# Sums over tokens and backward offsets placed among the exponents and inner products of the SSD outputs, exponent rows loaded in two halves

## The chip, the cores and the metric

The program runs on one core of a Trainium2 chip. The metric is the device time of one execution in microseconds; of several runs the median counts. The profile is of one execution, and its times are microseconds from the start of its span.

## What is computed

Two blocks run one after the other over 2048 tokens of width 1024. The first mixes by pooling and by a bidirectional state space scan (SSD), the second by a linear recurrence and by forgetting attention. The change touches only the stage that computes the outputs of the SSD. With 16 heads of width 64 in 4 groups, states of size 128 and chunks of 128 tokens, the reference says for each direction:

```python
acum = jnp.cumsum(adt, axis=2)
seg = acum[:, :, :, None] - acum[:, :, None, :]
decay = jnp.exp(jnp.where(lower, seg, -jnp.inf))
cb = jnp.einsum('bclgn,bcsgn->bclsg', cc, bc)
y_diag = jnp.einsum('bclsg,bclsgr,bcsgrp->bclgrp', cb, decay, xd)
chunk_states = jnp.einsum('bclgn,bclgr,bclgrp->bcgrpn', bc, decay_to_end, xd)
y_off = jnp.einsum('bclgn,bcgrpn,bclgr->bclgrp', cc, h_starts, jnp.exp(acum))
y = y_diag + y_off
```

and the output is `y_f + flip(y_b) + d_skip * xs`, multiplied by a gate. `h_starts` is the state at the start of each chunk: the state before times a decay, plus `chunk_states`.

## The kernel before

`ssd` goes over 16 chunks (`NC`), one function for each engine, and the order of the work on each engine is written out by hand. Semaphores are counted up by the steps and waited for by number. The backward states come from memory (`h_bwd`); the forward states are made here.

**TensorE, chunk c**, in its order of code:
- `products(c + 2)`: four 128x128 products of B and C into `psCB`, which is one of the two buffers of the exponents (`psE`). It waits until all exponentials of chunk c+1 are taken.
- `offset(c, hf)`: four products of 256 columns of C with the forward state into `psO`. It waits for `off_b_read`, since `psO` is one buffer and VectorE must have read the backward offsets of chunk c-1 from it.
- `skipped(0)`, a product of 512 columns with the identity into `psY`, then the inner products of heads 0 to 3 (`inside`, 64 columns each), and from there alternately `ahead(q)`, which is `exponents(c + 2, q)`, and two heads of `inside`. Each `exponents` is two products of 512 columns into `psE`: one over 10 rows (`seg_l`, `seg_r`), one with the masks. `skipped(1)` stands between `ahead(2)` and `ahead(3)`.
- `offset(c, hb)`, the same for the backward state, again into `psO`. It waits for `off_f_read`.
- `sums(c + 1)`, four products of 256 columns of B with the weighted inputs `xw` into `psS`. It waits for `weighted` (GpSimd), for the load of B, and for `state`: VectorE must have read `psS` of chunk c.

An fp32 product is recorded as two matmuls, so that the four of `offset` or `sums` are x8 in a row of the trace.

**VectorE, chunk c**: `state(c)` (line 919 decays the state into `y_tmp`, line 923 adds `psS` and counts up `state`), `decays(c + 1)` (lines 927 and 931, 2048 columns each), `forward(c)` (line 937 reads the forward offsets and counts up `off_f_read`; line 941 adds `psY`, once `inside` is counted up), `backward(c)` (line 944 reads the backward offsets, once `off_b` is counted up, and counts up `off_b_read`; line 948 adds them). In odd chunks line 964 follows, a piece of the next stage's weights.

**GpSimd, chunk c**: `weighted(c + 1)` (line 828), `gated(c - 1)` (line 838), in odd chunks a piece of weights (line 864), `skip(c + 1)` (line 834, which waits until `inside` of chunk c is done), and then `load_rows(c + 3)` (lines 841 and 843: three DMAs that bring the cumulated rows of both directions for the exponents). **ScalarE** takes the exponentials (line 888), copies `psCB` (line 877), and in odd chunks makes a part of the weights (line 909). **SyncE** issues the loads: `load_xs(c + 2)`, the inputs, when `inside` of chunk c is done, and the backward state of chunk c+2 when `off_b` of chunk c is.

## Time and profile before

| | us |
|---|---|
| median of 3 runs | 3515.5 |
| the runs | 3512.1, 3523.51, 3515.5 |
| the profiled execution, its own time | 3511.33 |
| its span | 3509.4 |
| TensorE busy in the span | 3265.5 (93%) |
| VectorE busy | 1642.1 (47%) |
| ScalarE, GpSimd busy | 962.8 (27%), 383.8 (11%) |
| granted TensorE clock, mean of the span | 0.95 |

The profiled execution is 4.2 us under the median and inside the spread of the runs; 1.9 us of its time lie outside the span. The granted clock is told as a share of full speed: 1.00 is 2.4 GHz, 0.50 is 1.2 GHz. Busy time of TensorE is not time at its peak, since matmuls are pipelined: a short matmul that waits for its weights counts as busy too.

### The profile page before, as it was taken

The page shows a single profiled execution, that of the slowest core. Times are in us where ns is not written, and L with a number is a line of the kernel's source. Part 1 is how long each engine was busy: PE and PEld are TensorE (multiplying, and loading weights), DVE is VectorE, ACT ScalarE, POOL GpSimd, SP SyncE. Part 2 cuts the span into 40 slices and gives each one's busy share as a digit, 9 for nine tenths or more (in the row PEclk, how much of TensorE's full clock was granted, in tenths as well). Part 3 has the DMA queues.
Part 4 walks back from the last instruction along what each step waited for, and adds up shares of the span by engine and source line. Part 5 has one row for each costly group of instructions (what it writes and reads, how often), then busy time and mean ns, then how long its engine had stood idle before and what let it go on. Part 6 is the DMA issues. An engine that isn't in the chain of part 4 may idle for free. (4 is left out here: it accounts for less than half of the span.)

```text
span 3509.4 us, 37796 instructions
## 1 busy us (share of the span) xinstructions
PE 3265.5 (93%) x15012; PEld 2564.9 (73%) x15012; DVE 1642.1 (47%) x1887; ACT 962.8 (27%) x1795; POOL 383.8 (11%) x246
## 2 busy tenths in 40 slices
PE   7899999997999979996999969999999699999788
PEld 7688888876888857765888858888877355555567
DVE  2754452466014237874444443243243665554355
ACT  2412221111210144532222231233223234433210
POOL 0100000000012035553000000000000201010012
PEclk9999999999999978987999989999999699999899
DMA  4222223332226355544333341222223312210232
GB/s 163 69 77 59 95 87 130 127 131 85 85 94 218 103 160 161 166 129 148 116 114 119 108 165 62 92 92 95 68 89 86 91 37 49 60 37 7 104 112 96
DMA packets 210926, 358.43 MB, mean 102 GB/s; under 512 B 22030, under 2 KB 143502, under 8 KB 202899
## 3 DMA queue, kind: packets, MB, share of 16 engines
q1 hardware_dynamic: 197782, 332.72, 29.3%
q10 hardware_dynamic: 5616, 17.97, 1.4%
q0 software_dynamic: 7392, 5.82, 0.8%
q8 instruction: 98, 1.61, 0.2%
q14 instruction: 38, 0.31, 0.0%
HBM read 234.57 MB, written 121.74 MB: 102 GB/s over the span
## 5 line engine op out<-in xcount | busy, mean ns | idle before, releaser
L636 PE MATMUL p_ps<-hmT_hi,p_w_hi 128*128 128x512 f32 x1312 | 525.5, 401 | 22.0 <-ACT p_work L356 16.4
L636 PE MATMUL p_ps<-hmT_hi,p_w_lo 128*128 128x512 f32 x1312 | 514.8, 392 | 0.0
L636 PE MATMUL p_ps<-hmT_lo,p_w_hi 128*128 128x512 f32 x1312 | 513.9, 392 | 0.0
L1748 PE MATMUL p_ps<-h2T_hi,p_w_hi 128*128 128x512 f32 x800 | 327.9, 410 | 19.2 <-DVE h2T_lo L1607 19.2
L1748 PE MATMUL p_ps<-h2T_hi,p_w_lo 128*128 128x512 f32 x800 | 315.6, 395 | 0.0
L1748 PE MATMUL p_ps<-h2T_lo,p_w_hi 128*128 128x512 f32 x800 | 315.4, 394 | 0.0
L636 PEld LDWEIGHTS p_ps<-hmT_hi,p_w_hi 128*128 128x128 f32 x1312 | 248.7, 190 | 75.9 <-issue 21.6
L636 PEld LDWEIGHTS p_ps<-hmT_hi,p_w_lo 128*128 128x128 f32 x1312 | 248.1, 189 | 53.4
L636 PEld LDWEIGHTS p_ps<-hmT_lo,p_w_hi 128*128 128x128 f32 x1312 | 248.9, 190 | 49.6
L1907 PE MATMUL t_psO<-t_prob,t_v 128*65 128x512 f32 (+3 forms) x640 | 262.0, 532 | 0.9
L1964 ACT ACTIVATE t_prob<-t_psS 128x1024 f32<-128x1024 f32 (+1 forms) x160 | 150.0, 938 | 317.7 <-PE t_psS L1895 179.5
L2002 DVE TENSOR_REDUCE t_chunk_max<-t_psM 128x1 f32<-128x512 f32 (+2 forms) x320 | 182.2, 606 | 94.9 <-PE t_psM L1878 70.0
L1748 PEld LDWEIGHTS p_ps<-h2T_hi,p_w_hi 128*128 128x128 f32 x800 | 153.0, 191 | 56.2 <-issue 24.6
L462 DVE COPY p_work<-p_ps 128x512 f32<-128x512 f32 (+3 forms) x93 | 55.6, 631 | 294.2 <-PE p_ps L656 260.5
L1748 PEld LDWEIGHTS p_ps<-h2T_lo,p_w_hi 128*128 128x128 f32 x800 | 152.6, 191 | 36.6 <-issue 6.0
L1748 PEld LDWEIGHTS p_ps<-h2T_hi,p_w_lo 128*128 128x128 f32 x800 | 152.4, 191 | 32.7
L1878 PE MATMUL t_psM<-t_KM,t_QB 66*128 66x512 f32 (+2 forms) x320 | 131.5, 479 | 27.2 <-DVE t_mask_k L2062 23.7
L1894 PE MATMUL t_psS<-t_QA,t_KA 128*128 128x512 f32 (+1 forms) x320 | 146.2, 457 | 9.3 <-DMA t_QB<-t_max_lo 9.2
L1907 PEld LDWEIGHTS t_psO<-t_prob,t_v 128*65 128x65 f32 x640 | 83.5, 138 | 96.5 <-issue 80.8
L1601 DVE TENSOR_TENSOR p_w_lo<-p_w_raw,p_w_hi 128x1024 fp32r<-128x1024 f32 x25 | 37.4, 1496 | 241.1 <-ACT p_w_hi L1503 241.1
L447 DVE TENSOR_TENSOR p_w_lo<-p_w_raw,p_w_hi 128x1024 fp32r<-128x1024 f32 x41 | 51.1, 1245 | 162.2 <-ACT p_w_hi L320 162.1
L1895 PE MATMUL t_psS<-t_QB,t_KB 68*128 68x512 f32 (+1 forms) x320 | 120.5, 376 | 0.0
(365 smaller groups left out, 5875.9 us busy)
## 6 DMA issues: line engine op xcount, KB each, us to landing
p_w_raw<-in_w_in SPq DMA_DIRECT2D x66, 512.0 KB, 6.0
p_spare<-in_wada ACTq DMA_DIRECT2D x32, 512.0 KB, 4.9
p_spare<-scratch_xs_tok SPq DMA_DIRECT2D x19, 512.0 KB, 4.4
scratch_xs_tok<-p_work SPq DMA_DIRECT2D x8, 1152.0 KB, 6.1
p_work<-in_wada SPq DMA_DIRECT2D x16, 512.0 KB, 3.4
p_work<-in_x SPq DMA_DIRECT2D x16, 512.0 KB, 3.3
scratch_dT<-p_work SPq DMA_DIRECT2D x8, 1024.0 KB, 5.9
scratch_zpT<-p_work SPq DMA_DIRECT2D x8, 1024.0 KB, 4.0
```

Source lines behind the costliest of these rows:

```text
L447: v.tensor_tensor(w_lo[b % 2][:], w_raw[b % 2][:], w_hi[b % 2][:].bitcast(F32), ALU.subtract).then_inc(S["w_lo"], 1)
L462: v.tensor_copy(tok_of(b)[:, 4 * g:4 * g + cnt, 0:width], tiles(PS[:, bank, :])[:, 0:cnt, 0:width]).then_inc(S["group_read"], 1)
L636: mm = pe.matmul(PS[:, c, 0:width], wt[n][:, q, :], xx[:, q, cols], start=(q == 0 and j == 0), stop=(q == KT - 1 and j == 2))
L1601: v.tensor_tensor(w_lo[b % 2][:], w_raw[b % 2][:], w_hi[b % 2][:].bitcast(F32), ALU.subtract).then_inc(S["w_lo"], 1)
L1748: mm = pe.matmul(ps[:, c, :], wt[n][:, q, :], xx[:, q, c * CH:(c + 1) * CH], start=(q == 0 and j == 0), stop=(q == KT - 1 and j == 2))
L1878: mm = pe.matmul(psM[:, m % 2, 0:w], QB[n][0:KM_ROWS, j * P:(j + 1) * P], KM[n][:, c * CH:c * CH + w], start=True, stop=not edge, skip_gro ...
L1894: pe.matmul(out, KA[n][:, ks], QA[n][:, qs], start=True, stop=False, skip_group_check=True)
L1895: mm = pe.matmul(out, KB[n][:, ks], QB[n][:, qs], start=False, stop=not edge, skip_group_check=True)
L1907: mm = pe.matmul(psO[:, o:CH], va[n][:, kt + e, 0:VD], pt[p % 2][:, e, o:CH], start=(kt + e == 0), stop=(kt + e == 4 * qc + 3), skip_group ...
L1964: act.activation(pt[p % 2][:, :, off:CH], psS[p % 2][:, :, off:CH], ACT.Exp, scale=1.0 / 8).then_inc(S["prob"], 1)
L2002: v.reduce_max(mx[:, j, c:c + 1], psM[:, m % 2, 0:w], axis=AX_X).then_inc(S["first_read"], 1)
```

## The change

The four products of `sums(c + 1)` no longer stand together at the end of chunk c. One stands after each of `ahead(1)`, `ahead(2)`, `ahead(4)` and `ahead(5)`; the first of them carries the waits. The four products of the backward offset are cut into two pairs, one before the last two heads and one after `ahead(7)`; the first pair carries the waits, the second counts up `off_b`. `load_rows` loads the rows of one direction at a time, and `exponents` waits for the first half at q = 0 and for the second at q = 4, each with its own semaphore. GpSimd issues the first half before `skip(c + 1)` (as soon as `ahead(3)` is done) and the second half after it.

```diff
@@ -754,10 +754,11 @@
         k = kit
         S = k.sems("y_", ("cb", "cb_copied", "weighted", "summed", "state", "seg", "exp", "skip",
                           "merged", "decays", "inside", "off_f", "off_f_read", "forward", "off_b", "off_b_read", "summed_y",
-                          "gated", "const", "lndt_in", "rows_in", "gate_in", "masks_in", "const_in", "seg_in", "z_in", "w_in", "w_gated", "w_hi",
+                          "gated", "const", "lndt_in", "rows_in", "gate_in", "masks_in", "const_in", "z_in", "w_in", "w_gated", "w_hi",
                           "w_lo"))
         bT_in, bt_in, x_in, h_in, y_out = ([k.sem(f"y_{what}{n}") for n in range(2)] for what in
                                            ("bT_loaded", "b_loaded", "xs_loaded", "hb_loaded", "stored"))
+        seg_in = [k.sem(f"y_seg_rows_loaded{n}") for n in range(2)]
         cT_in = [k.sem(f"y_cT_loaded{n}") for n in range(4)]
         dve = Tally(k.sem("y_dve_chain"))
         tokens = lambda t, c: t[c * P:(c + 1) * P, :]
@@ -836,22 +837,24 @@
                     g.wait_ge(S["summed_y"], c + 1)
                     g.wait_ge(S["z_in"], 16 * (c + 1))
                     g.tensor_tensor(y[c % 2][:], y[c % 2][:], zt[:], ALU.mult).then_inc(S["gated"], 1)
-                def load_rows(c):
-                    both = a["acum_rows"][:, c:c + 1]
-                    g.dma_start(seg_r[0:2, :], both.rearrange("m o h l -> m (o h l)")).then_inc(S["seg_in"], 16)
+                def load_rows(c, d):
+                    both = a["acum_rows"][:, c:c + 1, d * HEADS:(d + 1) * HEADS]
+                    g.dma_start(seg_r[0:2, d * HEADS * P:(d + 1) * HEADS * P],
+                                both.rearrange("m o h l -> m (o h l)")).then_inc(seg_in[d], 16)
                     for m in range(2):
-                        g.dma_start(seg_l[2 + 4 * m:6 + 4 * m],
-                                     both[m].rearrange("o (q j) l -> j (o q) l", j=4)).then_inc(S["seg_in"], 16)
+                        g.dma_start(seg_l[2 + 4 * m:6 + 4 * m, 4 * d:4 * d + 4],
+                                    both[m].rearrange("o (q j) l -> j (o q) l", j=4)).then_inc(seg_in[d], 16)
                 g.dma_start(seg_r[2:10], a["seg_r"][2:10]).then_inc(S["const_in"], 16)
                 g.dma_start(seg_l[0:2], a["seg_l"][0:2]).then_inc(S["const_in"], 16)
-                load_rows(0)
+                load_rows(0, 0)
+                load_rows(0, 1)
                 g.wait_ge(S["rows_in"], 80)
                 weighted(0)
                 skip(0)
-                g.wait_ge(S["seg"], 8)
-                load_rows(1)
-                g.wait_ge(S["seg"], 16)
-                load_rows(2)
+                for c in range(1, 3):
+                    for d in range(2):
+                        g.wait_ge(S["seg"], 8 * (c - 1) + 4 * d + 4)
+                        load_rows(c, d)
                 for c in range(NC):
                     if c + 1 < NC - 1:
                         weighted(c + 1)
@@ -862,11 +865,14 @@
                     if c % 2 == 1:
                         g.wait_ge(S["w_in"], 16 * (c // 2 + 1))
                         g.tensor_tensor(piece[:], piece[:], w.gate[:], ALU.mult).then_inc(S["w_gated"], 1)
+                    if c + 3 < NC:
+                        g.wait_ge(S["seg"], 8 * (c + 2) + 4)
+                        load_rows(c + 3, 0)
                     if c + 1 < NC:
                         skip(c + 1)
                     if c + 3 < NC:
                         g.wait_ge(S["seg"], 8 * (c + 3))
-                        load_rows(c + 3)
+                        load_rows(c + 3, 1)
                 gated(NC - 1)
             @block.scalar
             def _(act):
@@ -974,8 +980,8 @@
                         mm = pe.matmul(psCB[:, g, :], bT[c % 2][:, g, :], cT[c % 4][:, g, :], start=True, stop=True)
                     mm.then_inc(S["cb"], 1)
                 def exponents(c, q):
-                    if q == 0:
-                        pe.wait_ge(S["seg_in"], 48 * (c + 1))
+                    if q % 4 == 0:
+                        pe.wait_ge(seg_in[q // 4], 48 * (c + 1))
                     if q == 1:
                         pe.wait_ge(S["cb_copied"], c + 1)
                     elif 8 * c + q >= 2:
@@ -984,17 +990,19 @@
                               start=True, stop=False)
                     pe.matmul(psE[:, q % 2], ident_r[:], tri_r[:, q // 4].unsqueeze(1).to_broadcast([P, 4, P]), start=False,
                               stop=True).then_inc(S["seg"], 1)
-                def sums(c):
-                    pe.wait_ge(S["weighted"], c + 1)
-                    pe.wait_ge(bt_in[c % 2], 16 * (c // 2 + 1))
-                    if c >= 1:
-                        pe.wait_ge(S["state"], c)
-                    for g in range(GROUPS):
+                def sums(c, groups):
+                    if groups[0] == 0:
+                        pe.wait_ge(S["weighted"], c + 1)
+                        pe.wait_ge(bt_in[c % 2], 16 * (c // 2 + 1))
+                        if c >= 1:
+                            pe.wait_ge(S["state"], c)
+                    for g in groups:
                         mm = pe.matmul(psS[:, g * 256:(g + 1) * 256], bt[c % 2][:, g * NS:(g + 1) * NS],
                                        xw[:, g * 256:(g + 1) * 256], start=True, stop=True)
-                    mm.then_inc(S["summed"], 1)
-                def offset(c, state):
-                    for g in range(GROUPS):
+                    if groups[-1] == GROUPS - 1:
+                        mm.then_inc(S["summed"], 1)
+                def offset(c, state, groups=range(GROUPS)):
+                    for g in groups:
                         mm = pe.matmul(psO[:, g * 256:(g + 1) * 256], cT[c % 4][:, g, :], state[:, g * 256:(g + 1) * 256],
                                        start=True, stop=True)
                     return mm
@@ -1013,7 +1021,7 @@
                     for q in range(8):
                         exponents(c, q)
                     if c == 0:
-                        sums(0)
+                        sums(0, range(GROUPS))
                 pe.wait_ge(S["rows_in"], 80)
                 for c in range(NC):
                     ahead = (lambda q: exponents(c + 2, q)) if c + 2 < NC else (lambda q: None)
@@ -1030,25 +1038,29 @@
                     skipped(0)
                     inside(c, range(0, 4))
                     ahead(0)
+                    beside = (lambda g: sums(c + 1, (g,))) if c + 1 < NC - 1 else (lambda g: None)
                     inside(c, range(4, 6))
                     ahead(1)
+                    beside(0)
                     inside(c, range(6, 8))
                     ahead(2)
+                    beside(1)
                     skipped(1)
                     ahead(3)
                     inside(c, range(8, 10))
                     ahead(4)
+                    beside(2)
                     inside(c, range(10, 12))
                     ahead(5)
+                    beside(3)
                     inside(c, range(12, 14))
                     ahead(6)
+                    pe.wait_ge(S["off_f_read"], c + 1)
+                    pe.wait_ge(h_in[c % 2], 16 * (c // 2 + 1))
+                    offset(c, hb[c % 2], (0, 1))
                     inside(c, range(14, 16)).then_inc(S["inside"], 1)
                     ahead(7)
-                    pe.wait_ge(S["off_f_read"], c + 1)
-                    pe.wait_ge(h_in[c % 2], 16 * (c // 2 + 1))
-                    offset(c, hb[c % 2]).then_inc(S["off_b"], 1)
-                    if c + 1 < NC - 1:
-                        sums(c + 1)
+                    offset(c, hb[c % 2], (2, 3)).then_inc(S["off_b"], 1)
 def walk_tiles(eng, body, tally=None, per=0):
     body(0, 0)
     with eng.Fori(0, LT // 2 - 1) as i:
```

TensorE, from the skip product of a chunk to the second skip product. `psSeg` is the tile of the exponents, `psY` that of the inner and skip products, `psSt` that of the sums, `psO` that of the offsets. Before:

```order
4654 L1002 MATMUL psY<-y_xskip,ident 128x512
4655 L1006 MATMUL psY<-y_xs,y_decay_f 128x64 x4
4656 L983 MATMUL psSeg<-y_seg_r,y_seg_l 128x512
4657 L985 MATMUL psSeg<-y_masks_r,y_ident 128x512
4658 L1006 MATMUL psY<-y_xs,y_decay_f 128x64 x2
4659 L983 MATMUL psSeg<-y_seg_r,y_seg_l 128x512
4660 L985 MATMUL psSeg<-y_masks_r,y_ident 128x512
4661 L1006 MATMUL psY<-y_xs,y_decay_f 128x64 x2
4662 L983 MATMUL psSeg<-y_seg_r,y_seg_l 128x512
4663 L985 MATMUL psSeg<-y_masks_r,y_ident 128x512
4664 L1002 MATMUL psY<-y_xskip,ident 128x512
```

TensorE in the changed kernel, from the first inner products of a chunk to the same place:

```order
4642 L1014 MATMUL psY<-y_xs,y_decay_f 128x64 x4
4643 L989 MATMUL psSeg<-y_seg_r,y_seg_l 128x512
4644 L991 MATMUL psSeg<-y_masks_r,y_ident 128x512
4645 L1014 MATMUL psY<-y_xs,y_decay_f 128x64 x2
4646 L989 MATMUL psSeg<-y_seg_r,y_seg_l 128x512
4647 L991 MATMUL psSeg<-y_masks_r,y_ident 128x512
4648 L1000 MATMUL psSt<-y_xw,y_b 128x256
4649 L1014 MATMUL psY<-y_xs,y_decay_f 128x64 x2
4650 L989 MATMUL psSeg<-y_seg_r,y_seg_l 128x512
4651 L991 MATMUL psSeg<-y_masks_r,y_ident 128x512
4652 L1000 MATMUL psSt<-y_xw,y_b 128x256
4653 L1010 MATMUL psY<-y_xskip,ident 128x512
```

The first product of the sums now stands behind eight inner products and two exponents of its chunk, and everything that follows it in TensorE's queue waits for what it waits for.

TensorE, the end of a chunk and the start of the next. Before:

```order
4647 L1006 MATMUL psY<-y_xs,y_decay_f 128x64 x2
4648 L983 MATMUL psSeg<-y_seg_r,y_seg_l 128x512
4649 L985 MATMUL psSeg<-y_masks_r,y_ident 128x512
4650 L998 MATMUL psO<-y_hb,y_cT 128x256 x4
4651 L993 MATMUL psSt<-y_xw,y_b 128x256 x4
4652 L974 MATMUL psSeg<-y_cT,y_bT 128x128 x4
4653 L998 MATMUL psO<-y_hf,y_cT 128x256 x4
```

TensorE at the same place in the changed kernel:

```order
4667 L1006 MATMUL psO<-y_hb,y_cT 128x256 x2
4668 L1014 MATMUL psY<-y_xs,y_decay_f 128x64 x2
4669 L989 MATMUL psSeg<-y_seg_r,y_seg_l 128x512
4670 L991 MATMUL psSeg<-y_masks_r,y_ident 128x512
4671 L1006 MATMUL psO<-y_hb,y_cT 128x256 x2
4672 L980 MATMUL psSeg<-y_cT,y_bT 128x128 x4
4673 L1006 MATMUL psO<-y_hf,y_cT 128x256 x4
```

Between the last write of the backward offsets and the first write of the next forward offsets, both into `psO`, stood eight products; now four stand there, the small ones.

## Rows read from the trace of the kernel before

**Rows 1.** Busy time by stretch, the 13 chunks between two reads of backward offsets; columns first.
```profile
core 0: us, PE busy (x) PEld busy (x) DVE busy (x) ACT busy (x) POOL busy (x), PEclk, DMA share, GB/s
1293.90:1561.50 267.60, 267.50 (x1093) 196.37 (x1093) 207.67 (x111) 133.59 (x436) 152.49 (x84) 0.86 0.50 153
```

**Rows 2.** The same view, chunks 9, 10 and 11, each from skip product to skip product.
```profile
1464.70:1482.60 17.90, 17.90 (x86) 13.23 (x86) 15.95 (x9) 10.75 (x34) 13.38 (x7) 1.00 0.50 155
1482.60:1505.20 22.60, 22.60 (x86) 16.56 (x85) 17.62 (x12) 9.72 (x33) 9.37 (x7) 0.77 0.58 173
1505.20:1526.20 21.00, 21.00 (x85) 15.38 (x84) 13.72 (x7) 10.76 (x34) 15.04 (x9) 0.84 0.40 131
```

**Rows 3.** The same view, cut where the granted clock changes: chunk 7, then chunk 14.
```profile
1421.10:1430.10 9.00, 9.00 (x41) 5.72 (x39) 8.90 (x4) 5.34 (x20) 7.90 (x3) 1.00 0.59 175
1430.10:1440.40 10.30, 10.30 (x27) 7.83 (x27) 5.17 (x5) 4.81 (x15) 3.63 (x4) 0.50 0.28 69
...
1573.50:1577.00 3.50, 0.00 (x0) 0.00 (x0) 3.50 (x2) 0.00 (x0) 0.29 (x1) 0.50 0.00 0
```

**Rows 4.** Timeline of TensorE, chunk 9: start us, us, engine, line, instruction, tiles.
```profile
1464.75 1.02 PE L1002 MATMUL psY<-y_xskip,ident 128*128 128x512 f32 x2
...
1468.55 0.55 PE L1006 MATMUL psY<-y_xs,y_decay_f 128*128 128x64 f32 x4
...
1476.50 1.89 PE L998 MATMUL psO<-y_hb,y_cT 128*128 128x256 f32 x8
...
1479.95 1.05 PE L974 MATMUL psSeg<-y_cT,y_bT 128*128 128x128 f32 x8
1480.84 1.89 PE L998 MATMUL psO<-y_hf,y_cT 128*128 128x256 f32 x8
1482.57 1.02 PE L1002 MATMUL psY<-y_xskip,ident 128*128 128x512 f32 x2
```

**Rows 5.** Timeline at the tail, chunks 14 and 15; in brackets the idle time before.
```profile
1580.72 1.22 DVE L944 TENSOR_TENSOR y_tmp<-psO,y_eac 128x1024 f32<-128x1024 f32 x1 [2.39 <-PE psO L998]
...
1582.09 1.97 PE L998 MATMUL psO<-y_hf,y_cT 128*128 128x256 f32 x8 [1.41 <-DVE y_tmp L944]
```

**Rows 6.** Timeline of VectorE from the backward read of chunk 9.
```profile
1478.43 1.23 DVE L944 TENSOR_TENSOR y_tmp<-psO,y_eac 128x1024 f32<-128x1024 f32 x1 [1.28 <-PE psO L998]
...
1480.83 2.92 DVE L964 SCALAR_TENSOR_TENSOR wo_early_lo<-y_w_piece,cols,wo_early_hi 128x1024 fp32r<-128x1024 f32 x1
...
1487.10 1.22 DVE L923 TENSOR_TENSOR y_hf<-y_tmp,psSt 128x1024 f32<-128x1024 f32 x1
```

**Rows 7.** The same view from the backward read of chunk 7.
```profile
1438.60 1.23 DVE L944 TENSOR_TENSOR y_tmp<-psO,y_eac 128x1024 f32<-128x1024 f32 x1 [3.57 <-PE psO L998]
...
1441.00 1.28 DVE L964 SCALAR_TENSOR_TENSOR wo_early_lo<-y_w_piece,cols,wo_early_hi 128x1024 fp32r<-128x1024 f32 x1
...
1445.16 1.22 DVE L923 TENSOR_TENSOR y_hf<-y_tmp,psSt 128x1024 f32<-128x1024 f32 x1
```

**Rows 8.** The same view from the backward read of chunk 8.
```profile
1460.20 1.23 DVE L944 TENSOR_TENSOR y_tmp<-psO,y_eac 128x1024 f32<-128x1024 f32 x1 [3.57 <-PE psO L998]
...
1465.56 1.22 DVE L923 TENSOR_TENSOR y_hf<-y_tmp,psSt 128x1024 f32<-128x1024 f32 x1
...
1474.18 1.21 DVE L937 TENSOR_TENSOR y_out<-psO,y_eac 128x1024 f32<-128x1024 f32 x1
```

**Rows 9.** Timelines of GpSimd: chunks 7 and 9.
```profile
1441.40 2.64 POOL L828 TENSOR_TENSOR y_xw<-y_xs,y_wst 128x1024 f32<-128x1024 f32 x1 [3.92 <-PE psSt L993]
...
1475.96 1.90 POOL L834 TENSOR_TENSOR y_xskip<-y_xs,y_dskip 128x1024 f32<-128x1024 f32 x1 [3.85 <-PE psY L1006]
1480.27 2.40 POOL L828 TENSOR_TENSOR y_xw<-y_xs,y_wst 128x1024 f32<-128x1024 f32 x1 [0.67 <-PE psSt L993]
```

**Rows 10.** Loads of the tile y_xs, issued 14 times from 1291.3 to 1556.6.
```profile
DMA to landing us min/median/max: 3.3/3.5/5.0
```

**Rows 11.** Waits from 1281 to 1589: who waited, for whom, us in total, times, longest.
```profile
PEld psSeg L983 <- DMA y_seg_l<-scratch_acum_rows: 0.2, 1, 0.2
```

## The prediction

> **What bounds the kernel now.** I read the busy time by stretch first. In the 13 chunks between the backward read of chunk 0 and that of chunk 13 TensorE is busy for 267.50 of 267.60 us [rows 1], so the stage is TensorE's, and nothing there can be won by taking waits away. But the granted clock of the stretch is 0.86. Next the same view chunk by chunk: chunk 9 runs at clock 1.00 and takes 17.9 us, chunk 10 has 0.77 and takes 22.6, chunk 11 has 0.84 and takes 21.0, with the same work [rows 2]. This repeats every three chunks. Cut where the clock changes, chunk 7 shows 9.0 us at 1.00 and then 10.3 at 0.50, in which TensorE was never idle [rows 3]: the clock fell among the exponents and inner products, and came back during the long run of offsets, sums and products. So the prize is the clock. A low stretch of 10.3 us made chunk 10 dearer by 22.6 - 17.9 = 4.7 us, one of 21.0 - 17.9 = 3.1 us belongs to 0.16 x 21.0 / 0.5 = 6.7 us low: 0.46 us for each us at the low clock. Over the 13 chunks 0.14 x 267.6 / 0.5 = 75 us are low, which cost 75 x 0.46 = 34 us. That is the most that the change can take, and 13 chunks at 17.9 are 233 us. The other engines are next: VectorE is busy for 15.95 of 17.9 us in the full-speed chunk [rows 2].
>
> **The rows in halves** cost or bring nothing. TensorE waited for exponent rows 0.2 us in the whole stage [rows 11]. Three more issues by GpSimd in each chunk stand ahead of `skip`, where GpSimd idles anyway: 3.85 us before line 834 in chunk 9 [rows 9], against 1.7 us that three issues take (below). If that cover is gone, `skip` comes later by up to 1.7 us, and its 1.9 us have to be done before the next chunk's skip product, 1482.57 - 1475.96 = 6.6 us behind `inside` before and 4.7 after; the cover would have to fail by 2.8 us to cost anything. Zero, within 1 us.
>
> **The order on TensorE** adds no instruction. What it moves are waits, and I follow them from one point, the start of VectorE's read of the backward offsets (line 944), called T.
>
> (a) `psO` is one buffer. Before, 1.73 us of sums and 0.89 us of products stood between the backward offsets and the next forward offsets (1476.50 to 1479.95 is twice 1.73, then 1480.84 - 1479.95 [rows 4]), and they hid the read. Now only the products do. The tail shows that case bare: line 944 starts at 1580.72, the forward offsets at 1582.09, 1.37 us later [rows 5]. So they start at T + 1.37, and the skip product at T + 1.37 + 1.73 (1482.57 - 1480.84 [rows 4]) = T + 3.10. Before it was 1482.57 - 1478.43 = 4.14 after T, but with 1.73 us of sums in between, so 0.7 us of waiting is new in each chunk.
>
> (b) The first product of `sums(c + 1)` waits for line 923 of chunk c. It now stands where 1468.55 - 1464.75 = 3.80 us of the chunk are over [rows 4], that is at T + 6.90. VectorE's queue after T is lines 944, 948, after an odd chunk line 964, then 919 and 923. Line 923 ends at 1465.56 + 1.22 - 1460.20 = T + 6.58 without line 964 [rows 8]. With it there are two cases: T + 9.89 [rows 6] and T + 7.78 [rows 7]; of the six such chunks of the stretch four look like the first, two like the second. With 0.15 us for the semaphore (1580.72 + 1.22 to 1582.09 [rows 5]) TensorE waits 0 us in odd chunks, and 3.1 or 1.0 us in even ones. Before, the sums stood at the chunk's end, at 1478.23, 11 us behind line 923 of that chunk (1466.78), and this never showed. Behind the waiting product the whole rest of the chunk is queued: inner products, exponents, and so ScalarE, `inside`, and the loads that hang on it.
>
> Which of the two it is depends on GpSimd. Line 964 took 1.28 us where it began at 1441.00, before line 828 at 1441.40, and 2.92 us where it began at 1480.83, behind line 828 at 1480.27 [rows 6, 7, 9]; line 919 then queues in the same way. In the new order line 828 no longer waits for the sums. GpSimd is free at 1480.27 - 0.67 - 1475.96 = 3.64 us after `inside` [rows 9]; T is 2.47 - 0.86 = 1.61 us after it (1478.43 - 1475.96, less half a backward offset), so GpSimd is free at T + 2.0; the inputs, issued at about T - 1.7, land 3.3 to 5.0 us later [rows 10], at T + 1.6 to T + 3.3; line 964 comes at 1480.83 - 1478.43 = T + 2.40. Both orders will occur, and I take 2.0 us, the middle of 1.0 and 3.1. The Trainium skill (SBUF — State Buffer, Who interferes with whom) says that a VectorE instruction with two SBUF inputs contends with GpSimd's reads and that the first to issue holds the shared ports throughout; the 1.28 against 2.92 us agree. By it alone the landing decides, and early landings everywhere would make all six waits 3.1 us.
>
> (c) The first pair of backward offsets waits for line 937, which ends at 1474.18 + 1.21 - 1460.20 = T + 15.19 [rows 8]. The pair's place is T + 3.10 + 11.75 (1476.50 - 1464.75) - 1.2 for the last exponents and inner products (the 7.95 us from 1468.55 to 1476.50 are six such steps and a skip product of 0.9) + 1.73 for the sums = T + 15.4. No wait, but nothing to spare.
>
> The sum at full clock: from T to the next T are 3.10 + 3.80 + (1476.50 - 1468.55 = 7.95) + 1.73 + (1478.43 - 1476.50 = 1.93) = 18.5 us in odd chunks, and 20.5 in even ones (19.5 to 21.6). Seven odd and six even are 129.5 + 123.0 = 252.5 us against 267.6, a gain of 15.1 us, if the clock stays up.
>
> **Does it stay up?** Between the dense products no stretch is left as long as the one in which the clock fell before, so I expect odd chunks to hold it. In even chunks the idle 1 to 3 us stand right behind the first eight inner products and two exponents. The old clock fell with TensorE never idle there [rows 3]; in chunk 14 it was at 0.50 while TensorE idled [rows 3]. I know no row for exactly 1 or 3 us, so the ends are no fall and a fall in each. I take a fall in each even chunk, since idle time is less work still than what already made it fall. And the way back is now longer: the run of dense products that brought it back is cut to 0.86 + 0.89 + 1.73 + 0.86 us. The low stretch then is between the shortest before (6.7 us) and about 20 (from T + 8 to the next chunk's start); I take 13. Six of them cost 6 x 13 x 0.46 = 36 us. 252.5 + 36 = 288.5, that is 21 us slower than 267.6.
>
> **The other stages** are not touched. At the start the exponents of chunk 1 find their rows a little sooner, at the tail `inside` of chunk 14 is placed behind a pair of offsets; each is under 2 us, and of opposite sign.
>
> **Rivals.**
> - **A, the forecast:** waits in even chunks, and the clock falls at them. 21 us slower; with 1.0 us waits and 10 us low 7 x 18.5 + 6 x (19.5 + 4.6) = 274, 6 slower, with 3.1 and 20 us 7 x 18.5 + 6 x (21.6 + 9.2) = 314, 47 slower. For it: lines 964 and 919 stand on the way in every second chunk.
> - **B, faster:** the waits are there, but the clock holds through them, because dense products follow at once. Price: 252.5, so 15 us faster, from 21 (all waits 1.0 us) to 8.5 (all 3.1 us). It decides as soon as the stage has less than 15.1 / 0.46 = 33 us at the low clock, against 75 now. The Trainium skill (TensorE: Matmul & The Clock Gate, Why this matters for your kernels) ties a lost clock to idle gaps between bursts of matmuls and asks only to keep the engine busy; gaps of 1 to 3 us would by it do little. The trace disagrees already before, with 0.50 at no idle time [rows 3], so I trust it little here.
> - **C, no difference:** the falls move but stay short, because the dense products bring the clock back at the second skip product. Six of 6.7 us cost 18 us, and 252.5 + 18 = 271, 3 us slower.
> - **D, it doesn't do what it says:** the clock falls in odd chunks too, since the first 3.8 us of a chunk are as before. Then odd chunks cost 3 to 5 us more as well, and the stage ends near A's far end.
>
> **How the numbers follow.** A with D 0.5, C 0.2, B 0.3. The profiled execution took 3511.3 us, the median is 3515.5; 21 us more are 3532 and 3537, and I say 3535. The range goes from B with short waits, 3515.5 - 21 = 3494, to A's far end, 3515.5 + 47 = 3562. About 0.3% (10.5 us) is what this kernel's measurement can tell from no change. Faster than that is most of B, 0.27; within are C, the near end of A and a bit of B, 0.25; slower is the rest, 0.48.
>
> **What would show it.** Right: TensorE waits at the sums' first product for line 923 in six chunks of even number, 1.0 or 3.1 us each, and before the forward offsets for line 944, 0.5 to 0.8 us in each chunk; line 944 to line 944 takes 18.5 us in odd chunks; the stretch's clock is about 0.85 with the low parts starting behind those waits. Wrong: a clock over 0.94 in the stretch (B); no wait for line 923, which would mean that the inputs land so late that line 919 goes first; waits for the rows' halves or for `weighted`, which I priced at nothing.

## The result, and the profile after

The changed kernel takes 3557.8 us (median of 4 runs, 3550.1 to 3561.8), the kernel before 3516.5 us (4 runs, 3512.1 to 3523.5): a ratio of 1.0112 with a 95% interval of 1.0096 to 1.0128, so 41 us slower. The sign and the mechanism are those of the forecast; the size is a little over twice the 19.5 us that it gave. In its own profiled execution the span is 3552.1 us, 42.7 more than before.

In the changed file the lines are shifted: the state is decayed in line 925 (919 before) and updated in 929 (923), the forward offsets are read in 943 (937), the backward ones in 950 (944), the piece of weights is 970 (964); on TensorE exponents are 989 and 991, `sums` 1000 (993), offsets 1006 (998), skip 1010, inner products 1014 (1006); on GpSimd `weighted` is 829 (828).

Busy time by stretch, after, in the columns of [rows 1]: the 13 chunks from the first backward read, then chunks 7 to 10, each from skip product to skip product.

```profile
1295.40:1610.60 315.20, 293.23 (x1093) 208.04 (x1092) 212.88 (x110) 132.59 (x437) 169.57 (x122) 0.79 0.43 130
```
```profile
1447.60:1466.20 18.60, 18.14 (x85) 13.14 (x85) 14.81 (x9) 10.76 (x34) 13.78 (x10) 1.00 0.42 129
1466.20:1496.20 30.00, 26.65 (x86) 18.45 (x85) 16.74 (x10) 9.71 (x33) 10.97 (x10) 0.66 0.40 118
1496.20:1514.80 18.60, 18.14 (x86) 13.20 (x85) 16.31 (x9) 10.75 (x34) 15.23 (x11) 1.00 0.53 156
1514.80:1546.70 31.90, 29.01 (x85) 20.33 (x84) 17.63 (x10) 9.72 (x33) 12.06 (x11) 0.63 0.42 128
```

The 13 chunks take 315.2 us where they took 267.6 [rows 1]. Odd chunks hold the full clock in 18.6 us; the six even ones take 31.9, 29.4, 31.9, 30.0, 31.9 and 29.9 us at about 0.65. The pattern of three chunks [rows 2] is now one of two. The cut where the clock changes, as in [rows 3]:

```profile
1447.60:1470.80 23.20, 22.11 (x103) 15.64 (x102) 19.41 (x10) 12.49 (x41) 18.15 (x11) 1.00 0.53 159
1470.80:1491.20 20.40, 18.14 (x45) 12.33 (x45) 7.79 (x5) 6.24 (x23) 1.76 (x3) 0.50 0.19 64
1491.20:1522.00 30.80, 27.00 (x126) 19.66 (x127) 27.78 (x15) 14.77 (x47) 24.40 (x16) 1.00 0.65 193
1522.00:1545.80 23.80, 23.80 (x63) 16.67 (x62) 9.64 (x6) 7.44 (x25) 7.28 (x8) 0.50 0.23 71
```

These low stretches are 20.4 and 23.8 us long, twice the 10.3 us of [rows 3]. All six, one for each even chunk, are 17 to 24 us long and together 129.7 us (76.7 before, added up in the same way). The first one shown begins 0.6 us after TensorE stops for the wait described below (1470.17), the second 0.4 us behind the end of such a wait (1521.62). The waits of TensorE from 1281 to 1625, as in [rows 11]:

```profile
PE psSt L1000 <- DVE y_hf L929: 17.4, 6, 2.9
PE psO L1006 <- DVE y_out L943: 5.9, 1, 5.9
PE psSeg L980 <- ACT y_decay_b L894: 4.6, 10, 0.5
```

Six waits of 2.9 us for the state update, one in each even chunk; ten of 0.5 us for an exponential; one of 5.9 us, which lies at the tail. The timelines of TensorE, VectorE and GpSimd from the backward read of chunk 7 (1463.03) show how the long wait comes about:

```profile
1463.03 1.23 DVE L950 TENSOR_TENSOR y_tmp<-psO,y_eac 128x1024 f32<-128x1024 f32 x1 [0.42 <-PE psO L1006]
1465.43 2.92 DVE L970 SCALAR_TENSOR_TENSOR wo_early_lo<-y_w_piece,cols,wo_early_hi 128x1024 fp32r<-128x1024 f32 x1
1468.28 3.38 DVE L925 TENSOR_TENSOR y_tmp<-y_hf,y_cdec 128x1024 f32<-128x1024 f32 x1
1471.69 1.22 DVE L929 TENSOR_TENSOR y_hf<-y_tmp,psSt 128x1024 f32<-128x1024 f32 x1
```
```profile
1465.06 2.21 POOL L829 TENSOR_TENSOR y_xw<-y_xs,y_wst 128x1024 f32<-128x1024 f32 x1
```
```profile
1463.45 1.13 PE L980 MATMUL psSeg<-y_cT,y_bT 128*128 128x128 f32 x8 [0.46 <-ACT y_decay_b L894]
1464.42 1.95 PE L1006 MATMUL psO<-y_hf,y_cT 128*128 128x256 f32 x8
1466.20 1.02 PE L1010 MATMUL psY<-y_xskip,ident 128*128 128x512 f32 x2
1469.67 0.50 PE L991 MATMUL psSeg<-y_masks_r,y_ident 128*128 128x512 f32 x1
1473.06 1.19 PE L1000 MATMUL psSt<-y_xw,y_b 128*128 128x256 f32 x2 [2.89 <-DVE y_hf L929]
```

GpSimd's line 829 begins 0.37 us ahead of line 970. Line 970 then takes 2.92 us instead of 1.28 [rows 7], line 925 runs beside the next GpSimd instruction and takes 3.38, and the update ends 9.88 us after the backward read. TensorE comes to the first sum 2.9 us sooner. Line 829 was ahead in all six cases, by 0.37 to 0.38 us.

Where the 42.7 us of the span are: 1.5 ahead of the first backward read; 47.6 in the 13 chunks; 5.2 at the tail (from the read of chunk 13 to the first product of the next stage 55.2 us, before 50.0); together 54.3. Later stages, with the same code, gave 11.6 back. Most of that is one stretch, before first, then after:

```profile
2600.00:2715.30 115.30, 105.67 (x472) 85.67 (x471) 41.43 (x33) 34.79 (x39) 2.39 (x1) 0.93 0.31 90
```
```profile
2654.30:2759.60 105.30, 98.84 (x473) 80.26 (x472) 41.24 (x33) 34.79 (x39) 2.42 (x2) 1.00 0.34 99
```

In the profiles of this study, all with this code untouched, the time from that first product to the end of the span lies between 1886 us (after, 156 us of it at the low clock) and 1901 us (e10, 180 us of it). So single times are read here by the 13 chunks, not by the total.

### The profile page after: what moved, and what is told of

It is laid out like the page before. It is cut to its first block and busy times, and to the rows that moved or that the text cites. A ratio compares the mean times of both kernels' runs of the same rounds, so it can differ in the third digit from the quotient of the medians.

```text
span 3552.1 us, 37860 instructions
## 1 busy us (share of the span) xinstructions
PE 3281.8 (92%) x15012; PEld 2569.3 (72%) x15012; DVE 1645.8 (46%) x1887; ACT 962.9 (27%) x1795; POOL 406.4 (11%) x294
## 3 DMA queue, kind: packets, MB, share of 16 engines
q1 hardware_dynamic: 197782, 332.72, 29.1%
## 5 line engine op out<-in xcount | busy, mean ns | idle before, releaser
L1890 PE MATMUL t_psM<-t_KM,t_QB 66*128 66x512 f32 (+2 forms) x320 | 131.5, 479 | 27.2 <-DVE t_mask_k L2074 23.7
```

Of the source, the lines that this page charges most:

```text
L1890: mm = pe.matmul(psM[:, m % 2, 0:w], QB[n][0:KM_ROWS, j * P:(j + 1) * P], KM[n][:, c * CH:c * CH + w], start=True, stop=not edge, skip_gro ...
```

## The experiments

**The theories.** One: the wait for the state update lets the clock fall, and the spread order has no run of dense products that would bring it back, so that it stays low. Two: the spread order cannot hold the clock, wait or no wait. Three: the halves of the rows cost something. The table has for each kernel the 13 chunks, the time at the low clock in them, TensorE's waits for the state update in them (together, longest), and the time of the kernel; where no ratio is given below, that is a single run. The kernel before, run beside them, took 3517 to 3521 us. In all of them the exponents, offsets, sums, skip and inner products do the same work.

| kernel | 13 chunks | low | waits | time |
|---|---|---|---|---|
| before | 267.6 | 76.7 | none | 3516.5 |
| after | 315.2 | 129.7 | 17.4, 2.9 | 3557.8 |
| e4, one sum early | 316.3 | 156.4 | 12.4, 2.4 | 3554.2 |
| e6, sums only | 304.0 | 102.4 | 17.5, 2.9 | 3548.9 |
| e9, offsets only | 274.3 | 88.7 | none | 3515.6 |
| e2, piece later | 241.4 | 0 | none | 3484.3 |
| e11, the same | 241.4 | 0 | none | 3483.5 |
| e5, sums later | 244.0 | 0 | none | 3493.6 |
| e3, update twice | 271.1 | 54.6 | 5.1, 0.9 | 3508.0 |
| e3b, update three times | 278.4 | 51.2 | 12.6, 2.1 | 3518.7 |
| e12, run behind wait | 318.1 | 135.4 | 16.8, 2.9 | 3569.2 |
| e13, four behind wait | 295.5 | 88.7 | 16.2, 2.9 | 3538.3 |
| e1, rows whole | 353.2 | 194.6 | 5.0, 1.8; for rows 21.0, 3.8 | 3605.9 |
| e10, piece later, rows whole | 338.8 | 174.1 | none; for rows 23.1, 3.8 | 3591.7 |
| e7, no gap | 253.0 | 30.7 | 2.3 once; for `weighted` 2.1 once | 3491.1 |
| e8, no gap, load later | 238.4 | 0 | none | 3480.4 |

### Taking the wait away: e2, e11, e5

e2 moves line 970 of VectorE one chunk on, behind the read of the forward offsets, where nobody on TensorE's path waits for VectorE. TensorE's order is that of the change, word for word.

```diff
                                     ALU.mult).then_inc(S["off_f_read"], 1)
+                    if c >= 2 and c % 2 == 0:
+                        low_piece(c // 2 - 1)
                     v.wait_ge(S["off_f_read"], c + 1)
...
                     backward(c)
-                    if c % 2 == 1:
-                        q = c // 2
-                        v.wait_ge(S["w_hi"], q + 1)
-                        v.scalar_tensor_tensor(w.lo[:, q, :], piece[:], s.cols1[:, V_PSCALE + q:V_PSCALE + q + 1],
-                                               w.hi[:, q, :].bitcast(F32), ALU.mult, ALU.subtract).then_inc(S["w_lo"], 1)
+                low_piece(NC // 2 - 1)
```

`low_piece(q)` holds the lines that are taken out.

> The changed kernel with one edit on VectorE: the piece of weights (line 964 of the kernel before), which stood between the backward read and the state update after each odd chunk, is made one chunk later, between the reading of the forward offsets and the adding of psY, where VectorE idles. TensorE's order is that of the change. Theory 1 (the wait of TensorE for the state update makes the clock fall, and the spread order keeps it low): the update is over 6.6 us after the backward read in every chunk, before TensorE asks for it at 6.9, so the six waits of 2.9 us go, the clock stays at 1.00, every chunk takes 18.6 us, and the 13 chunks take 242 us where the changed kernel takes 315 and the kernel before 268: about 3485 us, 25 to 32 faster than before. Theory 2 (the spread order itself lowers the clock, the wait only comes with it): the waits go, but even chunks stay near 27 to 30 us, and the time stays over 3535. Theory 3 (the rows in halves or GpSimd's issues do it): nothing moves, about 3558.

Measured: 3484.3 us, ratio 0.989 (0.9866 to 0.9914). The stretch, TensorE's waits in it, and VectorE's update after the backward read at 1427.04:

```profile
1297.10:1538.40 241.30, 235.37 (x1092) 170.68 (x1092) 196.72 (x110) 132.81 (x436) 174.21 (x122) 1.00 0.54 169
```
```profile
PE psSeg L982 <- ACT y_decay_b L894: 6.0, 13, 0.5
```
```profile
1432.39 1.22 DVE L929 TENSOR_TENSOR y_hf<-y_tmp,psSt 128x1024 f32<-128x1024 f32 x1
```

The update ends 6.57 us after the backward read, 3.3 us sooner than in the change. No wait for the update, no fall, every chunk 18.57 us. TensorE is idle for 6 us here and was for 0.1 us before, and the stage is 26 us shorter: the clock outweighs the waits. e11 is the same kernel again.

> e2_piece_later once more, beside e8_no_gap_load_later on one chip, so that the two can be compared: 3484 within 6, all chunks at 18.57 us and clock 1.00 from the first to the thirteenth.

Measured: 3483.5 us, ratio 0.9905 (0.9882 to 0.9927), again 241.4 us with nothing low.

e5 leaves VectorE alone and lets TensorE come to the sums later: the second skip product and two more exponents stand ahead of the first one.

```diff
                     ahead(1)
-                    beside(0)
+                    skipped(1)
                     inside(c, range(6, 8))
                     ahead(2)
-                    beside(1)
-                    skipped(1)
                     ahead(3)
+                    beside(0)
+                    beside(1)
```

> The changed kernel with one edit on TensorE instead: the second skip product moves up behind the second exponents, and the first two products of the sums move down behind the fourth exponents; VectorE's order is that of the change. The first sum is then asked for 9.9 us after the backward read, where the state update has been over for 0 us (it ends at 9.9, plus 0.15). Theory 1: the waits shrink from 2.9 to about 0.2 us, the clock stays up, 13 chunks take 243 us, about 3487. Theory 2: low clock in even chunks as before the edit, over 3535. It differs from the other edit in that no instruction of VectorE moves, so both fast says that the wait is the cause and not where the piece of weights stands.

Measured: 3493.6 us, ratio 0.9917 (0.9889 to 0.9945), and no wait for the update.

```profile
1297.90:1541.90 244.00, 237.99 (x1092) 171.97 (x1092) 212.31 (x110) 131.46 (x437) 171.97 (x122) 1.00 0.55 168
```

Two ways to lose the wait, and both hold 1.00 in the spread order. Theory two has fallen.

### The wait by itself: e3 and e3b

Both are e2 with the state update (line 929) done two or three times over in even chunks from chunk 2 on, with the same value each time, so that only the last one counts up `state` (the line 929 is 931 here). The diff is that of e3 on e2; e3b has a 2 in the place of `1 if`.

```diff
+                    for n in range(1 if c >= 2 and c % 2 == 0 else 0):
+                        step(v.tensor_tensor(hf[(c + 1) % 2][:], tmp[:], psS[:], ALU.add))
                     v.tensor_tensor(hf[(c + 1) % 2][:], tmp[:], psS[:], ALU.add).then_inc(S["state"], 1)
```

> As e2_piece_later, but the state update is done twice in even chunks from chunk 2 on (the same values), so that it is over about 1.25 us later, 7.8 us after the backward read: TensorE waits about 1.1 us in each even chunk, in the place where the changed kernel waits 2.9. Theory 1 in the form of the prediction (any idle time in that place makes the clock fall): falls in most even chunks, each of 25 to 31 us. Theory 1 with a length from which it decides: no fall, even chunks 19.7 us, 13 chunks 249 us.

> e2_piece_later with the state update done three times in even chunks from chunk 2 on, so that TensorE waits about 2.1 us in each of the six, between the 0.9 us of e3_wait_one (falls in four of six) and the 2.9 us of the changed kernel (falls in six of six). If longer waits make the fall surer: falls in five or six, mean of the even chunks 27 us, about 3535. If the fall depends on where the wait lies in time more than on its length: four of six as with 0.9 us, about 3515.

Measured, the waits of e3 and then of e3b, with the stretch of each:

```profile
PE psSt L1004 <- DVE y_hf L931: 5.1, 6, 0.9
```
```profile
1296.10:1567.20 271.10, 260.96 (x1092) 186.21 (x1092) 203.74 (x116) 132.85 (x437) 171.72 (x122) 0.90 0.49 151
```
```profile
PE psSt L1004 <- DVE y_hf L931: 12.6, 6, 2.1
```
```profile
1296.60:1575.10 278.50, 260.26 (x1093) 184.32 (x1092) 207.50 (x123) 132.65 (x437) 175.92 (x122) 0.91 0.48 147
```

With waits of only 0.84 to 0.86 us the clock falls in four of the six chunks (28.3, 22.5, 28.3 and 22.6 us; the other two take 19.7). With waits of 2.1 us it falls in all six. The wait alone, in a kernel that otherwise holds 1.00, makes the fall: theory one's first half is shown. But the length of the low stretch doesn't grow with the wait: it is 20.5, 6.8, 0, 20.5, 6.8 and 0 us in e3, and 3.4 us in four chunks, 20.5 and 17.1 us in the two others of e3b. For e3b either 3535 us or 3515 us had been expected: the falls were six, as for the first, and the time was near the second, because four of them were short. What decides between 3 and 20 us after one and the same wait stays open.

### Which dense products matter: e6, e9, e4

e6 keeps the spread sums and puts the backward offsets back together at the end. e9 keeps the two pairs of offsets and puts the four sums together behind them. e4 keeps only the first sum early; the three others and the whole offsets stand at the end.

The diff is that of e9; e4 does the same with groups 1 to 3 and has the whole `offset(c, hb[c % 2])`, with its waits, ahead of them.

```diff
                     ahead(1)
-                    beside(0)
                     inside(c, range(6, 8))
                     ahead(2)
-                    beside(1)
                     skipped(1)
...
                     ahead(4)
-                    beside(2)
                     inside(c, range(10, 12))
                     ahead(5)
-                    beside(3)
                     inside(c, range(12, 14))
...
                     offset(c, hb[c % 2], (2, 3)).then_inc(S["off_b"], 1)
+                    for g in range(GROUPS):
+                        beside(g)
```

And that of e6:

```diff
-                    pe.wait_ge(S["off_f_read"], c + 1)
-                    pe.wait_ge(h_in[c % 2], 16 * (c // 2 + 1))
-                    offset(c, hb[c % 2], (0, 1))
                     inside(c, range(14, 16)).then_inc(S["inside"], 1)
                     ahead(7)
-                    offset(c, hb[c % 2], (2, 3)).then_inc(S["off_b"], 1)
+                    pe.wait_ge(S["off_f_read"], c + 1)
+                    pe.wait_ge(h_in[c % 2], 16 * (c // 2 + 1))
+                    offset(c, hb[c % 2]).then_inc(S["off_b"], 1)
```

> The changed kernel with the backward offsets whole again behind the last exponents; the sums stay spread and the rows in halves. Theory 1: the wait of 2.9 us in even chunks is the same and the clock falls there; the run of dense products at the chunk's end is 0.86 us longer, which brings the clock back a little sooner: low stretches of 17 to 20 us, 3540 to 3558. If the division of the offsets had the main part in the loss: 3525 or less.

> The changed kernel with the four products of the sums together again, behind the second pair of backward offsets; the backward offsets stay in two pairs and the rows in halves. Theory 1: no wait for the state update and none for the read of the backward offsets, 17.8 us in full-speed chunks. One pair of dense products stands before the last inner products, too late in the chunk to help, since the old clock fell 9.0 to 10.3 us after the skip product and the pair stands at about 10.9: the clock pattern stays that of the kernel before, 3515 to 3525. If the pair is enough to hold the clock: 13 chunks in 232 us, 3480.

> The changed kernel, but only the first product of the sums stays early, behind the second exponents, with its waits; the other three stand behind the backward offsets, which are whole and at the chunk's end as before. The wait for the state update is the same 2.9 us. Theory 1 (the wait makes the clock fall; how long it stays low is set by how long the run of dense products at the end is): the fall comes in every even chunk, but the run at the end is 1.7 + 1.3 + 0.9 + 1.7 + 0.9 us long, so the clock is back sooner, the low stretches are 14 to 20 us in place of 17 to 24, and even chunks take 27 to 29 us in place of 30 to 32. Rival: the spread products have no part in the length, even chunks 30 to 32. Odd chunks have no dense product between the first sum and the second skip product but otherwise the old order, and may fall as the kernel before did: then 21 to 23 us instead of 18.5.

Measured, the stretches of e6, of e9 and of e4:

```profile
1296.20:1600.20 304.00, 280.28 (x1092) 199.62 (x1091) 208.35 (x110) 133.15 (x436) 167.09 (x120) 0.83 0.44 135
```
```profile
1295.80:1570.10 274.30, 273.37 (x1094) 198.67 (x1093) 204.39 (x111) 132.91 (x437) 176.04 (x122) 0.84 0.49 149
```
```profile
1293.90:1610.20 316.30, 303.86 (x1093) 217.18 (x1093) 214.44 (x110) 133.60 (x436) 172.15 (x121) 0.75 0.41 130
```

e9 never waits for the update and is still like the kernel before, with 88.7 us low and TensorE busy for 273.4 of 274.3 us: without the spread sums the clock falls with no idle time ahead in nine cases of ten, as in [rows 3] (the tenth stands behind its one wait of 0.9 us). e6 has the same waits as the change, and its odd chunks hold the clock at 18.58 us. e4 has the wait without the cover: six of its seven odd chunks fall too (mostly 21.0 us with 6.8 us low) and its low time is the longest of the three.

The lengths came out in part as expected. In e4 the low stretches of the even chunks are 17.1 to 20.5 us and the chunks 27.2 to 29.7 us (14 to 20 and 27 to 29 expected). In e6, where 17 to 20 us were expected, they are 20.5 to 23.9 us in four even chunks and 6.8 us in two, all behind the same wait of 2.9 us. One of each:

```profile
1424.20:1431.00 6.80, 6.54 (x13) 3.68 (x13) 5.84 (x4) 1.14 (x4) 0.00 (x0) 0.50 0.32 94
1465.20:1489.10 23.90, 21.30 (x52) 14.60 (x53) 9.36 (x6) 7.69 (x28) 6.57 (x9) 0.50 0.27 84
```

So the sums among the exponents are what holds the clock, and the first of them is what brings the wait.

### The way back: e12 and e13

The prediction said that the clock stays low because the run of dense products is cut up. e12 puts `beside(0)`, `beside(1)` and `skipped(1)` in one run right behind the wait; e13 puts all four sums there.

The diff is that of e12.

```diff
                     beside(0)
-                    inside(c, range(6, 8))
-                    ahead(2)
                     beside(1)
                     skipped(1)
+                    inside(c, range(6, 8))
+                    ahead(2)
                     ahead(3)
```

> The changed kernel with the same wait of 2.9 us in the same place, but a run of dense products right behind it: the first two products of the sums and the second skip product stand together after the second exponents (1.7 us at full clock, 3.4 at half), the other two sums as in the change. Theory (the clock falls at the wait, and how long it stays low is set by how soon a run of dense products comes): low stretches of 3 to 10 us in place of 17 to 24, even chunks of 23 to 26 us in place of 30 to 32, 3510 to 3530. Rival (the low stretch lasts until the run at the chunk's end whatever stands between): even chunks stay at 28 us or more, over 3540. Between skip product and next sum the spread is thinner than in the change, so odd chunks may fall too: then over 3540 with low clock in odd chunks, and the question stays open.

> The changed kernel with the same wait, and all four products of the sums together right behind it (1.7 us at full clock), nothing of the sums between the later exponents. Theory: as above the clock comes back early in even chunks; behind the second skip product no dense product stands for about 5 us, as in the kernel before, so the clock falls again late in the chunk, also in odd ones: low stretches of 3 to 10 us in most chunks, 3520 to 3550. Rival: low stretches of 17 us or more in even chunks, over 3555.

Measured: chunk 10 of e13, cut where the clock changes, and the matmuls at the first change; last the low stretch of its chunk 2.

```profile
1506.20:1512.90 6.70, 3.96 (x19) 2.49 (x17) 6.67 (x3) 2.28 (x8) 4.36 (x2) 1.00 1.02 303
1512.90:1516.40 3.50, 3.35 (x8) 2.75 (x9) 3.43 (x3) 0.00 (x0) 0.00 (x0) 0.52 0.50 167
1516.40:1523.10 6.70, 6.70 (x29) 4.26 (x29) 2.29 (x2) 4.35 (x16) 1.76 (x3) 1.00 0.03 5
1523.10:1530.10 7.00, 7.00 (x22) 5.46 (x22) 2.32 (x2) 2.49 (x9) 4.12 (x5) 0.51 0.35 83
```
```profile
1513.05 3.63 PE L1000 MATMUL psSt<-y_xw,y_b 128*128 128x256 f32 x8 [2.89 <-DVE y_hf L929]
```
```profile
1325.30:1349.20 23.90, 22.43 (x57) 15.60 (x58) 9.34 (x7) 6.84 (x24) 5.88 (x8) 0.50 0.24 69
```

The clock falls at the wait as before, but with the four sums (3.63 us) right behind it is back after 3.5 us in five of the six even chunks, where the change needs 17 to 24 us in all six. In chunk 2, behind the same wait and with the same four sums, it stays low for 23.9 us; there it fell 1.5 us before the wait's end, in the five others in its last 0.4 us or right behind it. So with a run right behind the wait the stretch was mostly short and once was not, and e6 and e3b have short stretches (6.8 and 3.4 us) without such a run: the second half of theory one has e13 on its side and is not shown. Then the stretch behind the second skip product has no dense product left, and the clock falls again for 7 us with TensorE busy throughout; two odd chunks fall too, as expected. In e12 it is the same with the parts exchanged: from chunk 4 on 3.4 us, then 13.6 us, even chunks of 29.1 us, and nothing won. Its 3569.2 us lie where its rival had them and not at the 3510 to 3530 of the theory, since the theory had no second fall in even chunks. In both kernels the same sums could not be the run that brings the clock back and the cover that keeps it.

### The halves of the rows: e1 and e10

e1 is the change with the exponent rows loaded whole again (three DMAs and one semaphore instead of six and two); e10 is e2 with the same edit.

```diff
-                    if c + 3 < NC:
-                        g.wait_ge(S["seg"], 8 * (c + 2) + 4)
-                        load_rows(c + 3, 0)
                     if c + 1 < NC:
...
                         g.wait_ge(S["seg"], 8 * (c + 3))
-                        load_rows(c + 3, 1)
+                        load_rows(c + 3)
...
-                    if q % 4 == 0:
-                        pe.wait_ge(seg_in[q // 4], 48 * (c + 1))
+                    if q == 0:
+                        pe.wait_ge(S["seg_in"], 48 * (c + 1))
```

> The changed kernel with the exponent rows loaded whole again, by three DMAs and one semaphore, in the place of the kernel before; the order on TensorE is that of the change. Theory 1: the halves cost nothing, 3558 us within 5, waits for the state update of 2.9 us in six chunks, low clock in the even chunks. Theory 3 (the halves or their issues on GpSimd have a part in it): 5 us or more less than the changed kernel.

> e2_piece_later with the exponent rows loaded whole again (three DMAs behind skip, one semaphore). In e1_rows_whole TensorE waited up to 3.8 us for these rows at the first exponents of a chunk, and the clock fell behind that wait too. If the rows' lateness belongs to the order and not to VectorE's piece: waits of 2 to 4 us for the rows in some chunks, low clock in them, 3500 to 3560. If it came only from the disturbed chunks of e1_rows_whole: 3485.

Measured: e1 3605.9 us, ratio 1.0248 (1.0216 to 1.028); e10 3591.7 us. The stretch, the wait and its longest case in e1, then the wait in e10:

```profile
1301.50:1654.70 353.20, 323.56 (x1092) 227.22 (x1092) 209.65 (x111) 132.59 (x436) 149.81 (x86) 0.72 0.39 116
```
```profile
PE psSeg L983 <- DMA y_seg_l<-scratch_acum_rows: 21.0, 8, 3.8
```
```profile
1418.74 0.79 PE L983 MATMUL psSeg<-y_seg_r,y_seg_l 10*128 10x512 f32 x1 [3.79 <-DMA y_seg_l<-scratch_acum_rows]
```
```profile
PE psSeg L985 <- DMA y_seg_l<-scratch_acum_rows: 23.1, 8, 3.8
```

Theory three has fallen with the opposite sign: without the halves the change would be 48 us slower still, and e2 would lose more than it wins. In the spread order the time from GpSimd's issue of the rows to their first use is short: in e1 the last issue begins at 1411.35 and TensorE wants the rows at 1414.95, 3.6 us later, while their landing takes 5.7 us in the median (3.0 to 7.3). Before, in chunk 9, the last issue begins at about 1479.0 and the exponents at 1484.36, 5.3 us later, and the two loads landed after 4.4 and 5.0 us: it sufficed, by 0.3 us. The slow landings are not e1's own. Before, the median is 2.5 us, but every third chunk has 3.7 to 5.3 us like this one; and in the change the second halves, most of them issued 0.8 us behind the backward read, take up to 6.2 us while the first ones take about 2. The landings of chunk 9 before, then of the first and the second half in chunk 7 of the change:

```profile
DMA to landing us min/median/max: 4.4/4.7/5.0
DMA to landing us min/median/max: 1.9/2.0/2.1
DMA to landing us min/median/max: 4.8/5.2/5.6
```

The first half is issued 7.6 us sooner than the second (at 1455.72 in chunk 7 of the change), and the second, which lands late, isn't needed before the fifth exponents. That is what the halves are good for.

### Closing the last gaps: e7 and e8

e7 is e2 with `beside(3)` behind the second pair of backward offsets, where it covers the wait for the exponential, and `skipped(0)` ahead of the forward offsets, where it covers the read. e8 is e7 with SyncE's load of the piece of weights moved behind the other loads of its chunk.

```diff
                         products(c + 2)
+                    pe.wait_ge(S["skip"], c + 1)
+                    if c >= 1:
+                        pe.wait_ge(S["forward"], c)
+                    skipped(0)
...
-                    skipped(0)
                     inside(c, range(0, 4))
...
-                    beside(3)
                     inside(c, range(12, 14))
...
                     offset(c, hb[c % 2], (2, 3)).then_inc(S["off_b"], 1)
+                    beside(3)
```

> e2_piece_later (3484 us) with two edits on TensorE: the fourth product of the sums stands behind the second pair of backward offsets, and the skip product of the next chunk stands ahead of its forward offsets. Both fill the 0.75 us in which TensorE waits, once for the last exponential and once for the read of the backward offsets, in each chunk of e2_piece_later (18.57 us against 17.82 for the same work without waits). Theory 1: the clock holds, 17.85 us in each chunk, 9 to 10 us less than e2_piece_later over 13 chunks, about 3475. Against it: one dense product fewer between the fifth and the sixth exponents; if that is too few, low stretches come back, each 3 us or more.

> e7_no_gap with one edit on SyncE: in even chunks the load of the next piece of weights, which waits for VectorE's piece, is issued at the end of the loop and no longer ahead of the loads of the gate, the inputs and the states. In e7_no_gap the weighted inputs came late in two even chunks (line 828 began 6.2 us after the backward read in one, where 2.0 to 4.9 is usual), TensorE waited 2.1 and 2.3 us, and the clock fell for 6.8 and 23.9 us. If those late inputs were queued behind the piece, the waits and both low stretches go: 13 chunks at 18.07 are 235 us, 3474 to 3480, 6 less than e2_piece_later. If they came late for another reason, it is 3485 to 3495 like e7_no_gap.

Measured: e7 3491.1 us, ratio 0.9906 (0.987 to 0.9943); e8 3480.4 us, ratio 0.9894 (0.9874 to 0.9914). From e7 the two waits that are left and what is behind the second line; then chunks 8 and 9 of e8.

```profile
PE psSt L1002 <- DVE y_hf L929: 2.3, 1, 2.3
PE psSt L1002 <- POOL y_xw L829: 2.1, 1, 2.1
```
```profile
1410.48 2.86 POOL L829 TENSOR_TENSOR y_xw<-y_xs,y_wst 128x1024 f32<-128x1024 f32 x1 [4.20 <-DMA y_xs<-scratch_xs_tok]
```
```profile
1425.30:1443.40 18.10, 18.07 (x87) 13.11 (x85) 15.42 (x10) 9.72 (x33) 10.92 (x10) 1.00 0.53 163
1443.40:1461.90 18.50, 18.29 (x86) 13.05 (x85) 16.22 (x9) 10.75 (x34) 15.18 (x11) 1.00 0.60 189
```

e7 missed the 3475 us that were expected. Its chunks at full clock shrink from 18.57 to 18.07 us, but the sums come sooner, and twice TensorE waits, 2.1 us for GpSimd, which waited for its inputs, and 2.3 us for the update; the clock falls behind both, for 6.8 and 23.9 us. The profile of e7 is of the slowest of its four runs (3477.8 to 3498.1 us); what the others look like inside is not known. In e8 both waits are gone and the stage is the shortest of all, 238.4 us; not the 235 that were expected, because its odd chunks take 18.5 us. The inputs land after 3.3 to 4.1 us in e8, where they took up to 7.9 us in e7, and line 829 begins 2.0 us after the backward read in every chunk but the first, where in e7 it was up to 6.2: that speaks for the late inputs having queued behind the piece, with one profile on each side. Of the whole kernel e2, e11, e7 and e8 are 0.9 to 1.1% faster than before, and their intervals don't tell them apart.

## Why the prediction was right in sign and short in size

Step by step, in its order:

- **What bounds the kernel.** The clock, as read. e2 takes 26.2 us from the 13 chunks with 6 us more idle time. The most that the change could take was put at 34 us; e8 takes 29.2.
- **(a) The read of `psO`** was to cost 0.7 us in each chunk, 18.5 us in odd ones: 18.6 measured. One part was not named: `products` waits 0.5 us for the last exponential, ten times. It replaces the wait for the read, and the skip product comes at 1466.20 - 1463.03 = T + 3.17, for which 3.10 was forecast.
- **(b) The wait for the update** came where it was said, in the six even chunks, behind lines 964 and 919. Its size failed: the prediction took 2.0 us, the middle of two cases, and it was 2.9 in all six, 17.4 us instead of 12. It weighed the landings of the inputs evenly over 3.3 to 5.0 us; their median of 3.5 us [rows 10] already spoke for the short end, and line 829 begins at T + 2.03, ahead of T + 2.40, each time. By the Trainium skill (SBUF — State Buffer, Who interferes with whom) the first to issue holds the other up, which with early landings gave 3.1 us six times; the trace agrees, with line 829 first and line 970 at 2.92 us in all six.
- **(c) The backward pair** doesn't wait for line 943 in the 13 chunks. At the tail it does (below), as the whole offsets did before.
- **Does the clock stay up?** The fall in each even chunk and the clock held in odd ones are right, and so is what a low microsecond costs: with e2's 241.4 us as the full-clock case, (315.2 - 241.4 - 17.4) / 129.7 = 0.43 us, against 0.46. The failed step is the length of the low stretch. It was taken as 13 us, between 6.7 and about 20, and was 17 to 24 us. The number was the middle of a range and came from no row. The upper end was too low as well, by the prediction's own terms: from T + 8 to the next T are 20.5 - 8 = 12.5 us of work at full clock, and at 0.46 us lost for each low one they last 12.5 / 0.54 = 23 us. The reason that it gave, that the run of dense products is cut to pieces, is only in part borne out: with a run right behind the wait the stretch was 3.4 us in five cases of six (e13), but without one it was 6.8 us in two of six in e6 and 3.4 us in four of six in e3b. Why the change itself has no short one stays open. Six times 13 are 78 us against 129.7 us, and the missing 52 us at 0.43 to 0.46 are 22 to 24 us. With 5 us from (b) these are the 27 us between the 21 us of the sum and the stage's 47.6.
- **The other stages** were to add under 2 us with opposite signs. Start and tail added 1.5 and 5.2. The timeline of the tail in the changed kernel:

```profile
1624.68 2.08 PE L1006 MATMUL psO<-y_hb,y_cT 128*128 128x256 f32 x4 [5.94 <-DVE y_out L943]
1627.61 1.22 DVE L947 TENSOR_TENSOR y_out<-y_out,psY 128x1024 f32<-128x1024 f32 x1 [2.99 <-PE psY L1014]
```

  Before, the backward offsets of chunk 14 waited 6.04 us for line 937 in the same way, but all of `inside` stood ahead of them. Now the end of `inside` stands behind the first backward pair and its wait of 5.94 us, and line 947 waits for `inside`, where line 941 used to follow right on. The later stages gave 11.6 us back at the clock, which no row of the stage foretold.
- **The rows in halves** at nothing: true as far as it was asked, since they cost nothing. That the new order can't do without them was missed (e1: 48 us). The wait in [rows 11] was 0.2 us with the old distance; the step never asked what distance the new order leaves. (Three issues take 1.8 us, 0.58 and 1.19 in the GpSimd timelines; no row stood behind the 1.7.)
- **The rivals.** B, that the clock holds through the waits, fell: 0.85 us is enough in four of six (e3). C fell with the low stretches, which were about three times its 6.7 us. D fell: odd chunks hold 1.00. The Trainium skill (TensorE: Matmul & The Clock Gate, Why this matters for your kernels) by itself would have given B, since by it gaps of 1 to 3 us do little; the runs disagree, with falls at waits of 0.85 us (e3) and at no idle time at all (e9). That the clock held in e2 with 6 us of idle time in pieces of 0.5 is no argument against it.

The stage ended at A's far end, for which the prediction had 314 us (waits of 3.1 and 20 us low); it was 315.2, with waits of 2.9 and 21.6 us low in the mean.

## What to carry to other kernels

Dense products placed among thin ones can keep TensorE's clock up and win more than all the waits that they bring (26 us of 268 here), but each of them must come to inputs that are ready: a wait of 2.9 us at the first, in every second chunk, undid it and cost 74 us (315.2 against 241.4). Before moving such products forward, follow their oldest operand through every engine, with the slow case of each instruction on the way, and move what stands ahead of it (here one VectorE instruction, e2). And when work moves together, ask of every small load what distance is left between its issue and its use, and set against it the slowest landing in the trace and not the median.

## What the runs showed of the chip

- A wait of 0.85 us was enough for the clock to go from 1.00 to 0.50 in four chunks of six; waits of 0.5 us at another place, behind the backward pairs, never did (e2, 13 times).
- After one and the same wait of 2.9 us the low stretch was 3.4 us in five cases and 23.9 us in one where 3.6 us of dense products followed at once (e13, where one of the waits was only 1.7 us), and where they come one by one 17 to 24 us in all six (the change) or 6.8 us in two and 20.5 to 23.9 us in four (e6). What decides is open.
- A microsecond at the low clock cost 0.43 us in the change and in e13, 0.44 in e6, 0.45 in e3 and 0.48 in e3b: the stage less 241.4 us and less the waits, over the time at the low clock.
- The row loads landed in about 2 us or in up to 6 us, by where in the chunk they were issued: in chunk 7 of the change 1.9 and 2.1 us for the first half, and 4.8 and 5.6 us for the second, issued 0.8 us behind the backward read. In e1 the median was 5.7 us. What holds them up was not told apart.
- Stages with untouched code differed by up to 15 us between the profiles, with 25 us more at the low clock in the longest than in the shortest. A change under that size is read from its own stage.
